# Routing ahead of the first expert pass: where the first weight slabs are split, and where gates and pass table are computed

## The reference, cut to what matters

```python
def moe_swiglu(h, router_w, w_gate, w_up, w_down):
    t = h.reshape(B * L, D)                              # 256 x 1024
    logits = (t @ router_w).astype(jnp.float32)          # 256 x 8
    top_v, top_i = lax.top_k(logits, TOP_K)              # 2 of 8
    top_w = jax.nn.softmax(top_v, axis=-1)
    gates = jnp.sum(jax.nn.one_hot(top_i, N_EXPERTS) * top_w[..., None], axis=1)
    out = jnp.zeros((B * L, D), jnp.float32)
    for e in range(N_EXPERTS):
        out = out + gates[:, e:e + 1] * swiglu(t, w_gate[e], w_up[e], w_down[e])
```

## Time and profile before

| what | us |
|---|---|
| median of three runs | 1754.67 |
| lowest, highest | 1754.22, 1757.03 |
| profiled execution, first to last instruction | 1756.1 |
| busy in it: PE, PEld | 1682.2, 1426.2 |
| busy in it: DVE, ACT, POOL | 1306.9, 1031.5, 18.3 |
| read from HBM | 459.72 MB, 262 GB/s over the span |

### The profile page before, as it was taken

One profiled execution on the slowest core, in us unless ns is written; L12 is line 12 of the kernel. 1 busy time (PEld: TensorE's weight loads), 2 busy tenths in 40 slices (PEclk: granted clock), 3 DMA queues, 4 the chain that ended last, 5 costly groups with the idle time before them and its releaser, 6 DMA issues.

```text
span 1756.1 us, 23184 instructions
## 1 busy us (share of the span) xinstructions
PE 1682.2 (96%) x8662; PEld 1426.2 (81%) x8662; DVE 1306.9 (74%) x1111; ACT 1031.5 (59%) x900; POOL 18.3 (1%) x25
## 2 busy tenths in 40 slices
PE   6999999999997799799999999999999999999997
PEld 5998879998886588688878888888888788788785
DVE  6773645544565565588888888888888888988885
ACT  5342435543334443477767677677677677677673
POOL 1000000000000000000000000000000000000000
PEclk9997999999999899899999999999999999999999
DMA  8651535655553043689999999999879899899992
GB/s 308 210 175 52 188 96 170 190 174 195 173 202 120 1 140 142 220 310 365 351 348 366 350 340 371 323 363 375 318 286 366 317 363 376 316 379 341 340 375 114
DMA packets 222433, 461.42 MB, mean 263 GB/s; under 512 B 7314, under 2 KB 52580, under 8 KB 222388
## 3 DMA queue, kind: packets, MB, share of 16 engines
q1 hardware_dynamic: 221696, 459.53, 73.7%
q0 software_dynamic: 528, 1.22, 0.3%
q10 hardware_dynamic: 164, 0.04, 0.0%
HBM read 459.72 MB, written 1.05 MB: 262 GB/s over the span
## 4 chain that ended last, share of the span: by engine, by line
issue 59%; PE 34%; DVE 4%; ACT 2%; POOL 0%; DMA 0%; ACTq 0%; DVEq 0%; POOLq 0%
PE ps L1350 14%; PE ps L1336 13%; PE ps L1498 3%; PE ps L1459 1%; PE ps L1426 1%; PE ps L1445 1%; DVE w_lo L362 1%; ACT ta L659 1%; PE ps L1416 1%; DVE mx L1059 0%; DVE ta L1075 0%; POOL rstd L480 0%; DVE a_lo L792 0%; ACT a_hi L533 0%; DMA rows<-in_ev_conv_w 0%
## 5 line engine op out<-in xcount | busy, mean ns | idle before, releaser
L362 DVE TENSOR_TENSOR w_lo<-raw,w_hi 128x2048 fp32r<-128x2048 f32 x431 | 981.7, 2290 | 261.4 <-ACT w_hi L358 259.9
L358 ACT ACTIVATE w_hi<-raw 128x2048 fp32r<-128x2048 f32 x431 | 826.6, 1919 | 409.2 <-PE ps L1601 138.3
L1601 PE MATMUL ps<-w_hi,e_hi 128*128 128x512 f32 x896 | 354.2, 395 | 2.8 <-DVE e_lo L1201 2.8
L1601 PE MATMUL ps<-w_hi,e_lo 128*128 128x512 f32 x896 | 349.6, 390 | 0.0
L1601 PE MATMUL ps<-w_lo,e_hi 128*128 128x512 f32 x896 | 349.0, 389 | 0.0
L1601 PEld LDWEIGHTS ps<-w_hi,e_hi 128*128 128x128 f32 x896 | 168.3, 188 | 36.2 <-issue 3.0
L1601 PEld LDWEIGHTS ps<-w_hi,e_lo 128*128 128x128 f32 x896 | 168.2, 188 | 35.9
L1601 PEld LDWEIGHTS ps<-w_lo,e_hi 128*128 128x128 f32 x896 | 168.4, 188 | 33.5
L1623 PE MATMUL ps<-w_hi,at_hi 128*128 128x512 f32 x448 | 175.7, 392 | 1.9 <-DVE at_lo L1213 1.9
L1623 PE MATMUL ps<-w_lo,at_hi 128*128 128x512 f32 x448 | 175.1, 391 | 0.0
L1623 PE MATMUL ps<-w_hi,at_lo 128*128 128x512 f32 x448 | 174.9, 390 | 0.0
(11 more groups left out here) (273 smaller groups left out, 1701.4 us busy)
## 6 DMA issues: line engine op xcount, KB each, us to landing
raw<-in_moe_w_up SPq DMA_DIRECT2D x112, 1024.0 KB, 7.0
raw<-in_moe_w_gate SPq DMA_DIRECT2D x110, 1024.0 KB, 6.9
raw<-in_moe_w_down SPq DMA_DIRECT2D x110, 1024.0 KB, 6.5
raw<-in_xa_wkv SPq DMA_DIRECT2D x16, 1024.0 KB, 5.1
raw<-in_ev_w_in SPq DMA_DIRECT2D x14, 1024.0 KB, 8.6
raw<-in_od_w_in SPq DMA_DIRECT2D x12, 1024.0 KB, 5.1
raw<-in_ffd_w_gate SPq DMA_DIRECT2D x11, 1024.0 KB, 5.3
raw<-in_ffd_w_up SPq DMA_DIRECT2D x11, 1024.0 KB, 5.4
```

Of the source, the lines that this page charges most:

```text
L358: nc.scalar.activation(w_hi[:, n % CUT, :], at_, ACT.Copy).then_inc(hi_cut, 1)
L362: nc.vector.tensor_tensor(w_lo[:, n % CUT, :], place(n, r, behind)[0], w_hi[:, n % CUT, :].bitcast(F32), ALU.subtract).then_inc(lo_cut, 1)
L1601: mm = T.matmul(ps[:, bank, :], s, m, start=(h == 0 and k == 0 and j == 0), stop=(h == 1 and k == 3 and j == 2))
```

## The change

Work gets other places in the engines' programs, and one piece is rewritten:

1. `cut_hi(G0+1)` on ACT moves from behind both halves of the turning into the first half, ahead of that half's squares; `cut_lo(G0+1)` on DVE moves from ahead of the logits' copy to ahead of the second half's residual addition.
2. `cut_hi(G0+2)` moves ahead of the normed tokens; `cut_lo(G0+2)` moves from behind the table to behind the picks, ahead of the wait for the counts.
3. The gates and `pack_gates(0)` on DVE move from between picks and positions to behind `pack_lo(0)` and `cut_lo(G0+3)`, ahead of `cut_lo(G0+4)`.
4. The part of the pass table for the extra passes is computed for all three at once, on a row of 24 instead of three rows of 8: 12 operations for the table in place of 17.
5. ACT and DVE read the number of passes into a register only after the fifth pass (q = HP = 4), ahead of the loop over the later ones.
6. PE's first four slabs of a pass become a function `opening`; that of pass 0 stands before the loop, PE's register load behind it, and in the loop `opening(q)` stands under `If(q > 0)`, with `combine(q - 1)`.

On ACT:

```diff
                 turn_hi("moe", a_hi, tiles=range(4 * h, 4 * h + 4))
+                if h == 0:
+                    cut_hi(act, G0 + 1)
...
-            cut_hi(act, G0 + 1)
+            cut_hi(act, G0 + 2)
             act.wait_ge(n_rstd, NORMS["moe"] + 1)
...
-            cut_hi(act, G0 + 2)
             act.wait_ge(r_m, 1)
             nc.scalar.activation(lg[:, 9, 2:4], lg[:, 9, 0:2], ACT.Exp).then_inc(r_e, 1)
-            act.wait_ge(r_tab, 1)
-            n_pass = act.value_load(table[0:1, 0:1], min_val=NE, max_val=NE + 3)
...
             a_pass(HP, [(1, HB, False), (HB, HB + 1, None), (HB + 1, NB, True)])
+            act.wait_ge(r_tab, 1)
+            n_pass = act.value_load(table[0:1, 0:1], min_val=NE, max_val=NE + 3)
```

On DVE (the gates' seven operations are among the lines left out at either place):

```diff
             stage("o1", 3, {1: x_event(0, "o1"), 2: lambda: turn_lo("moe", a_hi, a_lo, tiles=range(4))})
+            cut_lo(dve, G0 + 1)
             dve.wait_ge(slab_used, FIRST["o1"] + 4)
...
-            cut_lo(dve, G0 + 1)
             dve.wait_ge(r_lt, 1)
             V.tensor_copy(logits[:, :], ps[0:NE, LOGITS, 0:256]).then_inc(r_ls, 1)
...
             V.tensor_tensor(mask, one1, one2, ALU.add).then_inc(r_cnt, 1)
-            dve.wait_ge(r_e, 1)
...
+            cut_lo(dve, G0 + 2)
             dve.wait_ge(r_ps, 2)
...
-            for k in range(3):
-                link(V.scalar_tensor_tensor(out=hit, in0=rk, scalar=float(k), in1=over, op0=ALU.is_equal,
-                                            op1=ALU.mult))
-                link(V.tensor_tensor(hit, hit, experts[0:1, NE:2 * NE], ALU.mult))
-                link(V.tensor_reduce(row16[:, 1, 8 + k:9 + k], hit, AX.X, ALU.max))
+            link(V.tensor_tensor(hit, rk3, which, ALU.is_equal))
+            link(V.tensor_tensor(hit, hit, over3, ALU.mult))
+            link(V.tensor_tensor(hit, hit, behind8, ALU.mult))
+            link(V.tensor_reduce(row16[:, 1, 8:11], hit, AX.X, ALU.max))
...
-            dve.wait_ge(r_tab, 1)
-            n_pass = dve.value_load(table[0:1, 0:1], min_val=NE, max_val=NE + 3)
...
-            cut_lo(dve, G0 + 2)
             pack_lo(0)
-            pack_gates(0)
-            for n in range(3, 6):
+            cut_lo(dve, G0 + 3)
+            dve.wait_ge(r_e, 1)
...
+            pack_gates(0)
+            for n in range(4, 6):
                 cut_lo(dve, G0 + n)
+            dve.wait_ge(r_tab, 1)
...
             v_pass(HP, [(1, HB, False), (HB, HB + 1, None), (HB + 1, NB, True)], None)
+            n_pass = dve.value_load(table[0:1, 0:1], min_val=NE, max_val=NE + 3)
```

On PE (`opening` holds the four `half_in` of G0 to G0+3):

```diff
             gather(0)
-            pe.wait_ge(r_tab, 1)
-            n_pass = pe.value_load(table[0:1, 0:1], min_val=NE, max_val=NE + 3)
-            with pe.Fori(0, n_pass) as q:
+            def opening(q):
                 pe.wait_ge(e_l, q + 1)
...
+            opening(0)
+            pe.wait_ge(r_tab, 1)
+            n_pass = pe.value_load(table[0:1, 0:1], min_val=NE, max_val=NE + 3)
+            with pe.Fori(0, n_pass) as q:
                 with pe.If(q > 0):
+                    opening(q)
                     combine(q - 1)
```

More of the change, by code:

```diff
@@ L180, in trunk_kernel @@
         table = sb("table", [1, 24], I32)
+        hits = sb("hits", [1, 3 * NE])
         with ExitStack() as s:
@@ L1175, in _ @@
             pack_tokens(0)
-            over, incl, rk, hit = (row16[:, i, 0:8] for i in range(4))
+            over, incl, rk = (row16[:, i, 0:8] for i in range(3))
             link(V.tensor_scalar(over, ps[0:1, 1, 16:24], float(BLK), None, ALU.is_gt))
@@ L1183, in _ @@
             link(V.tensor_copy(table[:, 1:1 + NE], experts[0:1, 0:NE]))
-            for k in range(3):
-                link(V.scalar_tensor_tensor(out=hit, in0=rk, scalar=float(k), in1=over, op0=ALU.is_equal,
-                                            op1=ALU.mult))
-                link(V.tensor_tensor(hit, hit, experts[0:1, NE:2 * NE], ALU.mult))
-                link(V.tensor_reduce(row16[:, 1, 8 + k:9 + k], hit, AX.X, ALU.max))
+            hit = hits[:, :].rearrange("p (k e) -> p k e", k=3)
+            over3, rk3 = (v.unsqueeze(1).broadcast_to([1, 3, NE]) for v in (over, rk))
+            which = experts[0:1, 0:3].unsqueeze(2).broadcast_to([1, 3, NE])
+            behind8 = experts[0:1, NE:2 * NE].unsqueeze(1).broadcast_to([1, 3, NE])
+            link(V.tensor_tensor(hit, rk3, which, ALU.is_equal))
+            link(V.tensor_tensor(hit, hit, over3, ALU.mult))
+            link(V.tensor_tensor(hit, hit, behind8, ALU.mult))
+            link(V.tensor_reduce(row16[:, 1, 8:11], hit, AX.X, ALU.max))
             link(V.tensor_scalar(row16[:, 1, 8:11], row16[:, 1, 8:11], float(NE), None, ALU.max))
             V.tensor_copy(table[:, 1 + NE:4 + NE], row16[:, 1, 8:11]).then_inc(r_tab, 1)
-            dve.wait_ge(r_tab, 1)
-            n_pass = dve.value_load(table[0:1, 0:1], min_val=NE, max_val=NE + 3)
             def column(k):
@@ L1230, in pack_gates @@
                 ins.then_inc(pg_rdy, 1)
-            cut_lo(dve, G0 + 2)
             pack_lo(0)
+            cut_lo(dve, G0 + 3)
+            dve.wait_ge(r_e, 1)
+            w1, w2 = lg[:, 9, 4:6], lg[:, 9, 6:8]
+            link(V.tensor_scalar(w1, lg[:, 9, 2:4], 1.0, None, ALU.add))
+            link(V.reciprocal(w1, w1))
+            link(V.tensor_tensor(w2, w1, lg[:, 9, 2:4], ALU.mult))
+            link(V.tensor_tensor(first, one1, wide(w1), ALU.mult))
+            link(V.tensor_tensor(left, one2, wide(w2), ALU.mult))
+            for b in range(2):
+                link(V.tensor_tensor(gate16[:, :, NE * b:NE * b + NE], first, left, ALU.add))
             pack_gates(0)
-            for n in range(3, 6):
+            for n in range(4, 6):
                 cut_lo(dve, G0 + n)
+            dve.wait_ge(r_tab, 1)
             def v_block(q, b, behind):
```

## The result

The changed kernel is slower: median 1785.71 us (1785.34 to 1787.09, four runs) against 1755.85 us (1754.22 to 1757.98, four runs) for the kernel before on the same chip, ratio 1.0166, interval 1.0152 to 1.018. The forecast was 1751.8 with a range up to 1754.6. It had the wrong sign, and it missed by 33.9 us, nine times the largest term of its sum (3.65).

A forecast was written before the change was run, and what follows sets the result against it. PE's back-to-back expert matmuls bound the kernel, so an earlier first pass ends it equally earlier. 3.65 + 0.3 - 0.9 = 3.0, rounded to 2.9: 1754.67 - 2.9 = 1751.8 us, range 1749.7 to 1754.6.

The forecast's parts named there:

- Part 1: Split of G0+1 moved on ACT and DVE: logits' copy at 725.87 instead of 729.52, gain 3.65 us.
- Part 2: Split of G0+2 moved into DVE's wait for the counts: cost 0, at worst 0.2 us.
- Part 3: End of the gather: gather stays at 5.83 us, fewer copies behind it before the first expert matmul, gain 0.3 us.
- Part 4: Gates come too late on DVE: G0+4 0.55 us late, whole lateness reaches PE at G0+6, loss 0.9 us.
- Part 5: Register loads moved on PE, ACT and DVE: cost 0, with bounds 0 and 0.4 us for PE's.
- Rivals E and F: E: stall at PE's skip over `opening(q)`, gain 0.6 us, chance 0.05. F: split of G0+1 doesn't hold logits, nothing, 0.03.
- Rival B: Clock falls once more between gather and G0, hiding the late gates: gain 0.9 to 3 us, typically 1.5; chance 0.14.
- Rival A: Clock stays up, so the gather takes 3.74 us: gain 5.0, 1749.7 us; chance 0.12.
- D: Late gates cost nothing, PE itself being behind or splits having more slack: gain 3.8, 1750.9 us; chance 0.17.
- Rival C: Slower: the same clock fall lasts, up to 27.3 us at half clock, 9.7 us net lost, 1764.4; chance 0.03.

The follow-up runs named there:

- e1: Changed kernel with the 96-byte tile `hits` allocated behind all others, so no tile's address differs from the kernel before: 1753.66 us, ratio 0.9982.
- e2: Kernel before with only an unused 96-byte tile added behind `table`: 1787.49 us, ratio 1.0174.
- e9: e1 with the gates and `pack_gates(0)` ahead of the split of G0+3 on DVE, not behind it: 1751.99 us, ratio 0.9976.
- e10: Kernel before with only the split of G0+1 moved, on ACT and DVE: 1754.01 us, ratio 0.9981.
- e12: e1 with `u` 64 bytes further; the edit also put `m_hi` and `m_lo` at a distance of 128: 1752.98 us, ratio 0.9972.
- e3: Changed kernel with `table` 16 wide instead of 24, so tiles behind `hits` move by 64 bytes: ratio 1.0084.
- e13: Kernel before with 256 unused bytes ahead of the expert part's tiles: ratio 0.9999.
- e4: Kernel before with an unused 32-byte tile behind `table`: 1779.41 us, ratio 1.0132.
- e6: Kernel before with 96 unused bytes ahead of the expert part's tiles alone: 1783.2 us, ratio 1.0155.
- e11: Kernel before with 128 unused bytes ahead of the expert part's tiles: ratio 1.0117.
- e15: Kernel before with 224 unused bytes ahead of the expert part's tiles: ratio 1.0138.
- e16: Kernel before with 192 unused bytes ahead of the expert part's tiles: ratio 1.0045.
- e5: Kernel before with an unused 96-byte tile ahead of all others, so operands keep their distances: 1756.61 us, ratio 1.0001.
- e14: Kernel before with `e_lo` alone moved by 96 bytes against the weights: 1771.33 us, ratio 1.0081.
- e8: Kernel before with `w_hi` and `w_lo` moved to 96 modulo 128, other large tiles left at 0: 1785.84 us, ratio 1.0173.

## Why the prediction was wrong

**The step that failed** is in its first paragraph: "A start of the first pass that comes x us earlier therefore ends the kernel x us earlier, unless PE then waits for something in the pass." That takes the pace of the matmuls behind as fixed. It was not, though PE waits no more than before and the clock, behind the first 3 us, stays at 1.00. The whole miss sits in the term that the sum did not have, the tile `hits`. It is sized by the kernels after and e1, which differ only in this tile's place. 4032 expert matmuls at the 6.84 ns of the six whole passes are 27.6 us. The 456 in feed-forward and memory add 3.1, together 30.7; e2, which adds nothing but an unused tile, says 30.6 by its ratio. Between the medians of after and e1 lie 32.0. From the first expert matmul to the end of the span after has 28.4 us more than e1 (1785.2 - 747.37 against 1751.4 - 741.97): the 27.6 and about 1.4 for seven matmuls at half clock, less 0.6 of DVE's lateness that these hide.

**The sum of the reordering was right in size.** With the addresses put back (e1), it foresaw 2.9 us less; the medians say 4.0, the interval 1.6 to 4.7. The profiled executions differ by 4.7 (1756.1 and 1751.4), but 1.6 of that is not the reordering: from the start of the eighth pass to the end before took 139.41 us and e1 137.79, since the fall of the clock at 1734.68 isn't in e1's trace. Step by step, e1 against before:

| step | forecast | e1 |
|---|---|---|
| residual addition to logits' copy (9.03 before) | -3.65 | 5.30: -3.73 |
| copy to gather (7.65) | 0 | 7.21: -0.44 |
| start of gather to first expert matmul (8.67) | -0.3 | 8.25: -0.42 |
| first expert matmul P to G0+6 (17.07) | +0.9 | 17.79: +0.72 |
| sum | -3.0 | -3.87 |

*Part 1* was right, in place and price. *Part 2*: cost 0, and 0.44 better, which the forecast had not. In e1 the clock fell at 731.0, after nearly all the counts, which then came every 0.225 us (a row of two) and not every 0.43; the gates are gone from ahead of the positions too. Two other traces part these. e9 has the gates gone and the counts at half clock, and takes 7.49 us (-0.16). e10 has the gates in place and the counts at full clock, and takes 7.85, DVE waiting 1.31 for ACT's exponential. So the new order alone gives 0.16, and 0.28 came with the later fall of the clock. With the counts that fast, e1's DVE goes from the split to the positions without a pause, which is what the prediction said would be late next. *Part 3*: the gather stayed at 5.86 us, as taken. *Part 4*: DVE began the split of G0+4 at P+9.21 and that of G0+6 at P+15.45, to 0.01 as forecast. PE took G0+4 at P+11.55 (forecast P+11.7), and the lateness at G0+6 was 0.72 of 0.92: of the 0.24 us behind the split, which the forecast read as no margin, 0.2 were one. e9 shows that the gates' place is the cause. *Part 5*: no register load or skip shows as a gap; the 0.16 us ahead of G0+4 has DVE's split behind it, and the passes before and behind the border at which ACT and DVE now load the register take 124.88 and 124.87 us in e1, like the others. Rivals E and F are out.

**Rival B** took place, but in some executions only: in the kernel after the clock is at 0.50 from 747.37 for 3.03 us, and P to G0+6 takes 19.22 us, 2.15 more than before (0.5 of it the slower pace); its own gain from residual addition to G0+6 is 2.27 where e1's is 3.87. In e1's the clock stayed up. Of the five profiles with the new order three have this second fall (after, e9, e12) and two don't (e1, e3); none of the thirteen others has it. The forecast gave it 0.14. Rival A did not happen: the clock fell later, but the gather kept its length. D is refuted by e1, where the late gates do cost 0.72. Rival C, my only way to a slower kernel, had the wrong mechanism: no long stretch at half clock opened behind the start.

**What I could have done.** I read the diff by its work and not by its allocations. No row of the trace of before shows a price for a moved tile, so it would have had to be bounded from both sides like any other unknown; even 1% on the pace of 4032 matmuls is 9 us, three times my whole sum. That the order's part of the forecast came out within 1 us helps nothing here: the range had no room for a term that was left out.

## What to carry to other kernels

Where PE is busy all the time, read its count of matmuls per stretch as well as its busy share, and ask of every change whether it moves a tile. Here the loaded and the streamed operand of back-to-back 512-column matmuls want to begin a multiple of 256 bytes apart; a new small tile goes last or is padded to 256 bytes (e1 and e13), and whether a change of allocation is neutral is checked with an unused tile of the same size. A slow result of a reordering should be taken apart into order and addresses before the order is blamed: here the one was worth 3 to 4 us, the other cost 30 to 32.

## What the runs showed of the hardware

- The pace of 128x512 matmuls depends on the distance of the two operands within a partition: 227.2 ns at a multiple of 256 bytes, 229.1 at 192, 232.3 to 234.2 at 32, 64, 96, 128 and 224 (e4, e3, e6, e11, e15, e16). Their common address does not matter (e5). The Trainium skill (TensorE: Matmul & The Clock Gate, Part 2: What happens when you issue a matmul) says that PE reads the streamed operand and the weights through two separate ports, so that a load takes no bandwidth from the running matmul. A pace that changes by 2 to 7 ns with the distance between the two doesn't fit with full independence; the measurement decides. What collides is not shown.
- The slowing spreads: with only `e_lo` at a bad distance, matmuls that don't use it slow from about 227 to between 231 and 234 ns (e14).
- At 256 columns a distance of 224 bytes made matmuls faster, 116.7 instead of 120.0 ns (e8).
- The clock was at half for the first 3 us of the expert passes in the profiles of after, e9 and e12 and at full in those of e1 and e3, though their engines' order there is the same or nearly so. A stretch of 27.3 us at half clock ahead of it, in the retention block, was 23.9 us in the profiles of e4 and e9. PE was busy throughout it.

Open: why only the distance counts, and why 64 bytes beyond costs more than 64 short; what e3's three short executions have; and how `e_lo` alone slows its neighbours in e14.
